# Triangular inverses of chunked linear attention: the two directions' products in antiphase, the backward one held in the other half of the partitions

## The reference, cut to what matters

```python
a_mat = beta[..., :, None] * jnp.einsum('nhcid,nhcjd->nhcij', k, k) * d_strict
rhs = jnp.concatenate([beta[..., None] * v, (beta * gam)[..., None] * k], axis=-1)
sol = lax.linalg.triangular_solve(a_mat, rhs, left_side=True, lower=True, unit_diagonal=True)
u0, w = sol[..., :dv], sol[..., dv:]
```

## Time and profile before

| | |
|---|---|
| median of 3 runs | 1996.61 us (1990.82 to 1996.77) |
| span of the profiled execution | 2001.2 us |
| PE busy | 1764.2 us (88%), 17970 instructions |
| DVE busy | 857.6 us (43%), 1514 instructions |
| ACT busy | 592.7 us (30%), 1018 instructions |
| POOL busy | 243.5 us (12%) |
| matmuls of `product` (`L525`) | 215.5 us, 6656 instructions |

### The profile page before, as it was taken

One profiled execution on the slowest core, in us unless ns is written; L12 is line 12 of the kernel. 1 busy time (PEld: TensorE's weight loads), 2 busy tenths in 40 slices (PEclk: granted clock), 3 DMA queues, 4 the chain that ended last, 5 costly groups with the idle time before them and its releaser, 6 DMA issues.

```text
span 2001.2 us, 44027 instructions
## 1 busy us (share of the span) xinstructions
PE 1764.2 (88%) x17970; PEld 1033.3 (52%) x17970; DVE 857.6 (43%) x1514; ACT 592.7 (30%) x1018; POOL 243.5 (12%) x270
## 2 busy tenths in 40 slices
PE   5998895977778877898999899999989998899996
PEld 2444543544444444445865784354447856853452
DVE  1567524111111111367666753151457747642331
ACT  3314521000000000334324424252253325424442
POOL 0002211111111111006112100001002103000001
PEclk8998996999999999998999999999999999999998
DMA  9758025999999999521000003110211000012101
GB/s 358 259 197 291 1 69 220 370 423 424 423 424 424 425 424 413 216 74 33 3 3 2 3 20 109 42 43 32 80 43 35 3 2 2 4 65 104 42 1 42
DMA packets 75098, 307.75 MB, mean 154 GB/s; under 512 B 10908, under 2 KB 22300, under 8 KB 57888
## 3 DMA queue, kind: packets, MB, share of 16 engines
q1 hardware_dynamic: 63280, 291.98, 37.2%
q0 software_dynamic: 5360, 9.33, 1.3%
q10 hardware_dynamic: 6272, 3.81, 0.6%
HBM read 301.01 MB, written 16.52 MB: 159 GB/s over the span
## 4 chain that ended last, share of the span: by engine, by line
PE 73%; DVE 13%; another core or an unknown queue 6%; ACT 4%; issue 3%; DMA 1%; DVEq 0%; ACTq 0%; POOL 0%; POOLq 0%
PE bank L2253 12%; PE bank L496 12%; PE bank L2269 6%; PE bank L1027 6%; PE bank L525 5%; PE bank L532 4%; PE bank L2091 3%; PE bank L2175 3%; PE bank L998 2%; DVE arena L1596 2%; ACT arena L1039 1%; PE bank L512 1%; PE bank L2115 1%; PE bank L2103 1%
## 5 line engine op out<-in xcount | busy, mean ns | idle before, releaser
L496 PE MATMUL bank<-hT,arena 128*128 128x512 f32 (+1 forms) x640 | 287.7, 605 | 3.6 <-ACTq L1040 2.4
L2253 PE MATMUL bank<-arena 128*64 128x256 f32 x1792 | 216.3, 399 | 66.9 <-remote 66.9
L525 PE MATMUL bank<-arena 64*64 64x64 f32 x6656 | 215.5, 220 | 22.7 <-DVE arena L1726 7.2
L525 PEld LDWEIGHTS bank<-arena 64*64 64x64 f32 x6656 | 203.8, 136 | 37.0 <-DVE arena L1726 10.1
L2253 PEld LDWEIGHTS bank<-arena 128*64 128x64 f32 x1792 | 135.6, 143 | 158.0 <-issue 107.8
L496 PEld LDWEIGHTS bank<-hT,arena 128*128 128x128 f32 (+1 forms) x640 | 122.9, 194 | 161.2 <-issue 156.6
L2859 DVE COPY arena<-bank 128x256 f32<-128x256 f32 x32 | 13.6, 425 | 329.6 <-PE bank L2261 329.6
L2269 PE MATMUL bank<-arena 128*64 128x512 f32 x448 | 104.0, 606 | 16.4 <-remote 16.4
L1027 PE MATMUL bank<-arena 128*128 128x512 f32 x256 | 110.4, 593 | 0.0
L1039 ACT ACTIVATE arena<-bank 128x512 f32<-128x512 f32 (+2 forms) x124 | 73.2, 590 | 118.9 <-PE bank L496 79.2
L532 PE MATMUL bank<-hT,arena 128*128 128x512 f32 x224 | 105.0, 607 | 1.7 <-remote 1.7
(11 more groups left out here) (448 smaller groups left out, 2677.1 us busy)
## 6 DMA issues: line engine op xcount, KB each, us to landing
arena<-w_gate SPq DMA_DIRECT2D x28, 2048.0 KB, 30.6
arena<-w_up SPq DMA_DIRECT2D x28, 2048.0 KB, 21.0
arena<-w_down SPq DMA_DIRECT2D x28, 2048.0 KB, 26.2
arena<-w_ada SPq DMA_DIRECT2D x12, 2048.0 KB, 19.7
arena<-w_in SPq DMA_DIRECT2D x10, 2048.0 KB, 11.7
arena<-w_out SPq DMA_DIRECT2D x6, 2048.0 KB, 7.6
arena<-w_in SPq DMA_DIRECT2D x6, 1536.0 KB, 6.9
hT<-w_up SPq DMA_DIRECT2D x4, 2048.0 KB, 20.9
```

What stands on the lines that cost most here:

```text
L496: m = pe.matmul(bank[b][0:w, :], slot2(n)[:, k, c:c + w], hT[:, k, :], start=(k == 0), stop=(k == KD - 1))
L525: m = pe.matmul(o[half(f), s, t], lhs[half(f), s, t], rhs[half(f), s, t], start=True, stop=True)
L2253: mm = pe.matmul(bank[b][c * CAP:(c + 1) * CAP, 0:FE // 2], XT[j][:, k % 4, k // 4, :], e_slot(e_at(e, i), KD)[:, k, c * (FE // 2):(c + 1) ...
```

## The change

The order of the products on PE is shifted by half a level: T of the forward direction goes with V of the backward one, and T of the backward one with V of the forward one of the next level. The two products of such a pair alternate matrix by matrix (`side_by_side`). So that they use different quarters, the backward direction's `Bn` and `T` are held in the other half of the partitions (a matrix with `f` = 0 in 64 to 127): its V product then goes from rows `1 - f` to columns `f`, its T product from rows `f` to columns `1 - f`. `Y` and `V` stay where they were. The first V of the forward direction and the last T of the backward one run alone.

For this, DVE writes the backward `Bn` and `Y` of level 0 half by half (`for to, at in ...`), and each backward transpose between `T` and `Y` becomes two transposes of 64 partitions (`turned_over`). In RWKV, ACT copies the backward `Bn` in two halves. Number, size and arithmetic of the matrix products are the same. DVE's fillers keep their place after the backward direction's step of a level. `levels`, `first_inverse` and `next_level` replace the code at the two call sites.

```diff
+            def side_by_side(*products):
...
+                for s in range(2):
+                    for t in range(TT):
+                        for b, lhs, rhs, rows, cols in products:
+                            o, lh, rh = pieces(bank[b]), pieces(lhs), pieces(rhs)
+                            for f in range(2):
+                                at, to = half(f ^ rows), half(f ^ cols)
+                                m = pe.matmul(o[to, s, t], lh[at, s, t], rh[at, s, t], start=True, stop=True)
...
+            def levels(t_full, y_full, v_full, Bn, T_, Y, V, banks_used=()):
+                def below(d, l):
+                    return (d, Bn[d], T_[d], d, 0)
+                def renewed(d, l):
+                    return (2 + d, Y[d], V[d], 0, d) if l < LEVELS - 1 else (2 + d, V[d], Y[d], 0, 0)
+                t_full[0].wait()
+                side_by_side(below(0, 1))[0].then_inc(sem("g_v_done0"), 1)
+                for l in range(1, LEVELS):
+                    v_full[0].wait()
+                    y_full[0].wait()
+                    t_full[1].wait()
...
+                    t0, v1 = side_by_side(renewed(0, l), below(1, l))
+                    t0.then_inc(sem("g_t_done0"), 1)
+                    v1.then_inc(sem("g_v_done1"), 1)
+                    v_full[1].wait()
+                    y_full[1].wait(2 if l > 1 else 1)
+                    if l < LEVELS - 1:
+                        t_full[0].wait()
+                        t1, v0 = side_by_side(renewed(1, l), below(0, l + 1))
+                        v0.then_inc(sem("g_v_done0"), 1)
+                    else:
+                        t1, = side_by_side(renewed(1, l))
+                    t1.then_inc(sem("g_t_done1"), 1)
...
-                    for l in range(1, LEVELS):
-                        for d in range(2):
-                            t_full[d].wait()
-                            product(d, g_Bn[d], g_T[d]).then_inc(sem(f"g_v_done{d}"), 1)
-                        for d in range(2):
-                            v_full[d].wait()
-                            y_full[d].wait()
...
+                    levels(t_full, y_full, v_full, g_Bn, g_T, g_Y, g_V, (2, 3))
...
+                        for to, at in (((slice(0, P), slice(0, P)),) if d == 0 else ((half(1), half(0)), (half(0), half(1)))):
+                            chain.mark(act.activation(pieces(r_Bn[d])[to], products[at, :, :, 0, :], ACT.Copy))
...
+                def turned_over(dst, src, done=None):
+                    for f in range(2):
+                        m = dve.transpose(dst[half(1 - f)], src[half(f)])
...
+                def first_inverse(d, Bn, Tm, Y):
+                    m = merged(d, 0, True).bitcast(F32)
+                    for to, at in (((slice(0, P), slice(0, P)),) if d == 0 else ((half(1), half(0)), (half(0), half(1)))):
+                        chain.mark(dve.tensor_tensor(blocks(Y)[to], blocks(Bn)[at], m[at], ALU.mult))
+                    chain.wait()
+                    chain(dve.tensor_tensor(blocks(Y), blocks(Y), over_blocks(const2("I64")), ALU.add))
+                    dve.sem_inc(sem(f"g_y_full{d}"), 1)
+                    if d == 0:
+                        chain(dve.transpose(Tm, Y))
+                    else:
+                        turned_over(Tm, Y)
+                    dve.sem_inc(sem(f"g_t_full{d}"), 1)
...
+                def next_level(d, l, Tm, Y):
+                    t_done[d].wait()
+                    if l < LEVELS - 1:
+                        dve.copy_predicated(blocks(Tm), merged(d, l, False), blocks(bank[2 + d])).then_inc(sem(f"g_t_full{d}"), 1)
+                        n_t[d] += 1
+                        dve.wait_ge(sem(f"g_t_full{d}"), n_t[d])
+                        if d == 0:
+                            dve.transpose(Y, Tm).then_inc(sem("g_y_full0"), 1)
+                        else:
+                            turned_over(Y, Tm, "g_y_full1")
...
-                        chain(dve.scalar_tensor_tensor(two(g_Bn[d]), kk, -1.0, two(g_V[d]), ALU.mult, ALU.mult))
...
+                        for to, at in (((slice(0, P), slice(0, P)),) if d == 0 else ((half(1), half(0)), (half(0), half(1)))):
+                            chain.mark(dve.scalar_tensor_tensor(two(g_Bn[d])[to], kk[at], -1.0, two(g_V[d])[at], ALU.mult, ALU.mult))
+                        chain.wait()
+                        first_inverse(d, g_Bn[d], g_T[d], g_Y[d])
```

More of the change, by code:

```diff
@@ L729, in rwkv_chunks @@
                         pe.wait_ge(bank_free[b], 1)
[L730 to L741, removed]
+                    levels(t_full, y_full, v_full, r_Bn, [r_bt[:, ct, d] for d in range(2)], [r_kmt[:, ct, d] for d in range(2)],
+                           [r_kr[:, ct, d, 0] for d in range(2)])
                     if ct == 1:
@@ L1524, in convolve @@
                         dve.sem_inc(sem(f"conv_full{i % 2}"), 1)
+                def turned_over(dst, src, done=None):
+                    for f in range(2):
+                        m = dve.transpose(dst[half(1 - f)], src[half(f)])
+                        if done is None:
+                            chain.mark(m)
+                        else:
+                            m.then_inc(sem(done), 1)
+                    if done is None:
+                        chain.wait()
                 def shift_both(i):
@@ L1593, in dve_second @@
                         for d in range(2):
-                            t_done[d].wait()
-                            if l < LEVELS - 1:
-                                dve.copy_predicated(blocks(g_T[d]), merged(d, l, False), blocks(bank[2 + d])).then_inc(sem(f"g_t_full{d}"), 1)
-                                n_t[d] += 1
-                                dve.wait_ge(sem(f"g_t_full{d}"), n_t[d])
-                                dve.transpose(g_Y[d], g_T[d]).then_inc(sem(f"g_y_full{d}"), 1)
-                            else:
-                                dve.copy_predicated(blocks(g_Y[d]), merged(d, l, True), blocks(bank[2 + d])).then_inc(sem(f"g_y_full{d}"), 1)
+                            next_level(d, l, g_T[d], g_Y[d])
                         if l in (2, 3):
```

39 lines of the change are left out of this document (15 added, 24 removed).

## The result

| | before | after |
|---|---|---|
| median | 1996.69 us | 2102.55 us (2101.06 to 2105.93) |
| ratio | | 1.0532 [1.0514 to 1.0549] |
| span of the profiled execution | 2001.2 us | 2103.9 us |
| ten inverses, first to fifth copy of each | 180.4 us | 250.6 us |

What follows compares the result with a forecast made beforehand. PE was taken to bound the inverses, DVE close behind; levels 22.7, starts 5.7, tails 3.7 and clock 8 sum to +40 us: 2041 in the profiled span, 2037 as median, range 2009 to 2060.

Steps and rivals of the forecast that it cites:

- rival 2: Paired bursts: four quarters run as two pairs, each burst 0.93 us longer, 2086 us; chance 0.06 together with rival 4.
- Its rule: PSUM writes of the new bursts: tiles of different rows cannot write the same PSUM bank at the same time.
- Rival 4: Paired products: they queue one after the other instead of alternating, then as rival 2; chance 0.06 together with it.
- Rival 1: Backward half transposes on DVE: half price, the two together cost one; about 2012 us; chance 0.12.
- Rival 3: DVE's backward half fits under the burst if what follows the backward copy takes under 1.2 us; 1990 us; chance 0.08.
- the clock: PE gaps before bursts released by the backward copy: half clock adds 0.93 us a burst; +8 us, bounds 0 and 17.
- the step on the starts: Ahead of each inverse's levels: halved backward first steps and an extra ACT copy delay the start; +5.7 us, bounds 2 and 10.
- 6.5 and 9.1 us of fillers: DVE's extra work per inverse, waits included: 6.5 in layer 0's first GDN inverse, 9.1 in its second RWKV-priced fillers entry.
- Levels: Merging levels of the ten inverses: 1.98 us forward plus 2.05 us backward plus fillers each; +22.7 us.
- Tails: End of each inverse: last backward T runs alone, +0.92 us where the fourth level has no fillers, four times; +3.7 us.
- The signs to look for: In the levels: copies 2.0 and 2.05 us plus fillers apart, PE idling released by DVE, DVE busy some 40 us longer.
- The one sign named against the four quarters: Paired bursts: if they take 2 us at a granted clock of 1.00, the four quarters are mis-sized.

Runs made afterwards that it cites:

- run with one turn: The no-gap run's kernel without the second half transpose of each backward level (half of the backward results wrong): 2038.49 us, ratio 1.0209.
- no-gap run: The changed kernel with wide unread products on PE behind the bursts, behind the first V and behind the first burst of an inverse: 2060.32 us, ratio 1.0320.
- two-quarter run: The changed kernel's order with the backward matrices in their usual half of the partitions, no half transposes, bursts on two quarters: 2073.72 us, ratio 1.0395.

## Why the prediction was right and wrong

**Right: the sign, and its reason.** Copy, burst, copy, burst is one chain, PE idles behind DVE before each burst, and the fillers all stand on it. The run with one turn shows the loss with the clock held and without the second transposes. The burst was right too: 64 instructions in 1.16 us, so rival 2 falls. Its rule (the Trainium skill, "TensorEngine Tiling (Array Packing)", Gotcha 1: PSUM Pressure) is not borne out for this pattern: each bank is written from both row halves in one burst, in different halves of the partitions, and 64 instructions take 1.16 us at clock 1.00, where two quarters take 2.08. Rival 4 falls with it. Rival 1 falls by the group of line 1548: 706 ns for 64 partitions, 712 for 128. Rival 3 falls by its own point of decision: 1.45 us of transposes behind the backward copy, over 1.2.

**Wrong: the size, by the clock.** That step looked for single long gaps inside the levels, took two of 2.6 and 2.7 us with different ends, and priced one slow burst behind each of 18 long gaps at half: +8, at most 17. It gave no price to the gaps of 0.9 us, nor to PE's wait in front of the levels, which the step on the starts took as covered but for 0.35 us in four of them. In the trace the clock falls in eight inverses at that wait or just behind it (2.57 to 3.45 us in five of them, 1.3 in three) and in the two second RWKV inverses amid gaps of at most 1.1 us. In all ten it does not come back while the rhythm lasts. Then 0.82 us are paid in every forward half level and 0.64 in the backward ones without fillers, and not 0.93 once per long gap in the backward ones, where the fillers cover it. Sized from the two traces: with the half levels of the no-gap run (2.06 forward; 2.24, or what the fillers make of it, backward) the 40 levels would take 214 us, and they took 250.6: **+36**. The last half levels are 22.3 against 13.4 in that run, +9, and the short stretches behind the inverses, whose u products start at half clock (61 of line 640 in 3.51 us, where it was 2.02), 127.1 against 121.2, +6. Together some **51 us where 8 stood**. The difference of the spans of the two runs, 45.6, is the same sum less what the added work costs.

**Wrong by less: the terms at the full clock.** 102.7 - 51 leaves 52, where 32 were forecast.
- Levels +34 (214 - 180.4), forecast 22.7 (its 6.5 and 9.1 us of fillers are 6.4 and 9.0 by its own terms, which changes 0.3 us in all). The forward half level is 2.06, not 1.98: from the copy's start to the burst 0.88 (1200.16 to 1201.04), where 0.79 was taken from a PE that idled only 0.22 us. The backward one is 2.24, not 2.05: the half transposes were priced at 0.64, the interval between starts of whole ones, and two of them take 1.45. In 40 levels that is 40 x 0.08 + 40 x 0.19 = 11.
- Tails +4.8 (8.6 to 13.4 in the no-gap run), forecast 3.7.
- Starts and what lies between the inverses: +12 in the no-gap run, forecast 5.7. The stretches in front of the second and third GDN inverse of layer 0, where 0.35 each was forecast because projections and evictions cover the rest, grow by 2.3 and 1.6 there. The two-quarter run has +5.1 here, without halved first steps and without added work. How the other 7 divide between the halved first steps and the added work was not taken apart.

**The signs to look for.** The copies did follow at 2.06 and 2.24 us at the start of the second RWKV inverses and at 2.88 elsewhere; levels of the second GDN inverse took 5.8 us, outside the 4.0 to 4.9 named, and those of the first RWKV inverse 6.8 to 8.1 (5.7 to 7.0 named). PE's idle time was released by DVE, as named (90 of 124 us in front of line 536). DVE is busy 54 us more, named 40. The one sign named against the four quarters, bursts of 2 us, did come, but at a clock of 0.50 and not at 1.00; a look at the clock in the same row keeps the two causes apart.

## What to carry to other kernels

Before a change makes the products shorter than what lies between them, ask what fills the gaps: a phase in which two engines take turns loses their overlap, and here it lost the granted clock as well, so the faster bursts ran at the old speed. Price the clock by the rhythm of a whole stage and by the wait in front of it, not only by its longest inner gap, and let it weigh on every burst of the stage and on the stage behind it. A half-height operation on DVE cost what the whole one did here (transposes 706 and 712 ns, `scalar_tensor_tensor` 688 and 686), so a split is one more instruction at full price. Work added to keep PE busy needs few, wide instructions, since PE's stops in the added work were waits for instructions.

## What was not expected of the hardware

- The clock fell from 1.00 to 0.50 in a steady rhythm of bursts of 1.16 us and gaps of 0.9 to 1.1 us (both second RWKV inverses), and in the other eight inverses, where a longer wait in front had cost it, the same rhythm kept it at 0.50. One code on two quarters held 1.00 through one inverse and 0.50 through another (15.52 and 21.37 us).
- PE stops for 0.2 to 2.0 us with no wait in the profile ("issue") when many small matmuls come close together: 43 times, 32.2 us, with bursts of 64 plus 24 and more small products of added work, 67 times, 40.3 us, with the doubled products, and only 14 and 12 times, 9.4 and 5.6 us, when the added work has few wide instructions. Every one of these 136 stops ends 1.2 to 1.6 us after a 16 KB transfer of instructions has landed.
